# A hybrid decoder layer: first products on inputs that are not yet normed, and a readout placed later

## The reference, cut to what matters

```python
h = rmsnorm(x, g_pre_mix)                 # x * rsqrt(mean(x*x) + eps) * g
proj = einsum('btd,de->bte', h, w_in) + b_in
u_a, u_g, q, k, v, o, ig, fg, gate_conv, gate_m = split_in(proj)
u = u_a * sigmoid(u_g)                    # GLU, feeds a depthwise convolution of width 31
...
# per head (4): chunkwise mLSTM memory C (512 x 256), normaliser n, running max m,
# driven by the gate rows ig and log_sigmoid(fg)
hm = hm * rsqrt(mean(hm*hm) + eps) * g_mh * sigmoid(o)
mix = sigmoid(gate_conv) * y_conv + sigmoid(gate_m) * y_m
x = x + rmsnorm(mix @ w_o, g_post_mix)
ff = square(relu(rmsnorm(x, g_pre_ff) @ w_ff1 + b_ff1)) @ w_ff2 + b_ff2
x = x + rmsnorm(ff, g_post_ff)
```

## Time and profile before

| | us |
|---|---|
| median of 3 runs | 1249.0 (1248.9 to 1249.25) |
| profiled execution, its own time | 1248.76 |
| its span, first to last instruction | 1247.3 |
| TensorE busy in it | 1234.6 |
| VectorE, ScalarE busy | 717.3, 498.6 |
| first product matmul begins | 15.88 |
| last GLU chunk ends | 120.2 |

### The profile page before, as it was taken

The page is one execution under the profiler, slowest core; times in us unless marked ns, Lnnn a source line. Parts: engine busy times, 40 slices in busy tenths (PEclk is TensorE's granted clock), DMA queues, the critical chain, the costliest instruction groups (busy, mean ns, idle before and its releaser), DMA issues.

```text
span 1247.3 us, 23524 instructions
## 1 busy us (share of the span) xinstructions
PE 1234.6 (99%) x9043; PEld 1159.9 (93%) x9043; DVE 717.3 (58%) x1032; ACT 498.6 (40%) x764; POOL 62.5 (5%) x128
## 2 busy tenths in 40 slices
PE   8999999999999999999999999999999999999998
PEld 7999978888797888879999999999999999999998
DVE  6342678887877888788455443338453122443334
ACT  5332443453354335335543222247554223444221
POOL 4011001101100110110000000000000000000000
PEclk9999999999999999999999999999999999999999
DMA  6235316514450651442323222331323222223222
GB/s 207 79 119 180 105 34 237 202 44 163 172 181 34 235 196 50 154 177 77 99 85 102 85 84 84 145 105 43 112 91 101 85 84 85 84 85 101 85 67 72
DMA packets 40357, 141.23 MB, mean 113 GB/s; under 512 B 4804, under 2 KB 7236, under 8 KB 40184
## 3 DMA queue, kind: packets, MB, share of 16 engines
q1 hardware_dynamic: 28888, 99.37, 23.6%
q0 software_dynamic: 11424, 41.23, 9.4%
HBM read 118.31 MB, written 22.26 MB: 113 GB/s over the span
## 4 chain that ended last, share of the span: by engine, by line
PE 95%; DVE 1%; DMA 1%; ACT 1%; issue 0%; DVEq 0%; SPq 0%; POOL 0%; POOLq 0%; ACTq 0%
PE product L1542 88%; PE side L1542 7%; DMA out_c_s<-crg 1%; DMA x<-in_xT 1%; DVE crg L1253 0%; DVE accp L1133 0%; ACT sqh L755 0%; PE side L1700 0%; DMA crg<-in_c_in 0%; DVE hm L1277 0%; DVE sqacc L1282 0%; SPq L389 0%; ACT whi L559 0%; PE product L1690 0%; DVEq L1133 0%
## 5 line engine op out<-in xcount | busy, mean ns | idle before, releaser
L970 DVE TENSOR_TENSOR wlo<-wraw,whi 128x1024 fp32r<-128x1024 f32 x176 | 215.2, 1224 | 222.9 <-ACT whi L559 218.9
L1542 PE MATMUL product<-ahi,whi 128*128 128x256 f32 x1520 | 320.4, 290 | 4.1 <-DVE alo L995 3.9
L1542 PE MATMUL product<-ahi,wlo 128*128 128x256 f32 x1520 | 317.2, 288 | 0.0
L1542 PE MATMUL product<-alo,whi 128*128 128x256 f32 x1520 | 314.9, 287 | 0.0
L559 ACT ACTIVATE whi<-wraw 128x1024 fp32r<-128x1024 f32 x176 | 184.4, 1052 | 254.8 <-PE product L1542 183.9
L1542 PEld LDWEIGHTS product<-ahi,whi 128*128 128x128 f32 x1520 | 244.7, 188 | 11.8 <-issue 6.2
L1542 PEld LDWEIGHTS product<-alo,whi 128*128 128x128 f32 x1520 | 245.3, 188 | 0.0
L1542 PEld LDWEIGHTS product<-ahi,wlo 128*128 128x128 f32 x1520 | 243.9, 188 | 0.0
L1133 DVE SCALAR_TENSOR_TENSOR accp<-u,wdw,accp 128x512 f32<-128x512 f32 x240 | 163.4, 745 | 0.3
L1542 PE MATMUL product<-hidhi,whi 128*128 128x288 f32 (+1 forms) x512 | 111.2, 289 | 0.0
L1542 PE MATMUL product<-hidlo,whi 128*128 128x288 f32 (+1 forms) x512 | 110.8, 288 | 0.0
(11 more groups left out here) (297 smaller groups left out, 1599.8 us busy)
## 6 DMA issues: line engine op xcount, KB each, us to landing
wraw<-in_wstream SPq DMA_DIRECT2D x176, 512.0 KB, 3.4
crg<-in_c_in POOLq DMA_DIRECT2D x32, 512.0 KB, 6.6
out_c_s<-crg POOLq DMA_DIRECT2D x32, 512.0 KB, 2.9
hb<-head_rows POOLq DMA_DIRECT2D x4, 580.0 KB, 5.3
x<-in_xT SPq DMA_DIRECT2D x4, 544.0 KB, 5.1
sgm<-in_xT SPq DMA_DIRECT2D x1, 2176.0 KB, 8.3
out_c_p<-cst POOLq DMA_DIRECT2D x4, 512.0 KB, 8.2
out_yT<-y SPq DMA_DIRECT2D x4, 288.0 KB, 2.2
```

The source lines that it names most:

```text
L970: V.tensor_tensor(wlo[:, k % RING, :, :], wraw[:, k % 2, :, :], whi[:, k % RING, :, :].bitcast(f32), ALU.subtract).then_inc(lo_done, 1)
L1542: return pe.matmul(out, lhsT, rhs, start=start, stop=stop, skip_group_check=check)
```

## The change

- **Start.** New operands `ghi` and `glo` are the two parts of x * g, without the root. ScalarE makes `ghi` with `g_pre_mix` as its scale, VectorE `glo` in one instruction. They feed chunks 0 to 7 and the gate rows. The first weight chunk and `col` are loaded ahead of x, the second weight chunk after half of it.
- **Order on TensorE.** Twenty warm-up matmuls; then chunks 0 and 1 in turns of four, two and two tiles; chunk 2 goes into `side` and has the column sums of the squares behind its third tile. All squares are made by ScalarE and added by VectorE.
- **Eviction.** For chunks 0 to 7 VectorE multiplies the product by `rst` out of PSUM (`gate_scaled`, `up_scaled`), ScalarE takes the sigmoid from SBUF (`gated`), VectorE makes the GLU product from SBUF (`up_gated`). The gate rows are multiplied by `rst` in `gate_logits`.
- **Meanwhile** the normed operands `ahi` and `alo` are made in between; TensorE waits for all of them ahead of chunk 8. A sigmoid is taken once right behind the root for its table.
- **POOL** waits for chunk 7's end ahead of the first load of head rows, bias and states, since `ghi` and `glo` lie in that memory.
- **Heads.** `weighted(0)` runs ahead of `readout(1)`, with its square ahead of the chain of L736 and `update(4)` behind its sum; `pv0` and `cu4` swap places in `USES`, hence slots.

The diff, cut to its core (allocation, semaphore names and the removed helpers `operands`, `two_products` and `sum_of_squares` left out):

```diff
 
 USES = ["q0", "q1", "k0", "k1", "v0", "kts", "v1", "v2", "v3", "v4",
         "o0", "cu0", "cu1", "o1", "cu2", "cu3", "o2", "o3",
-        "cu4", "pv0", "cu5", "pv1", "cu6", "pv2", "cu7", "pv3"]
+        "pv0", "cu4", "cu5", "pv1", "cu6", "pv2", "cu7", "pv3"]
 USES_HEAD = len(USES) // 2
 
 BY_CHUNK = {"q0": 0, "q1": 1, "k0": 2, "k1": 3, "v4": 7, "o0": 8, "o1": 9, "o2": 10, "o3": 11}
@@ -206,6 +206,8 @@
         wkp = at("wkp", [P, ST], f32)
...
@@ -385,11 +389,16 @@
         @block.sync
         def _(sp):
             stream = wstream.rearrange("(n s) p k m -> n s p k m", s=2)
+
+            def first_chunk(s):
+                sp.dma_start(wraw[:, s, :, :], wstream[s, :, :, :]).then_inc(raw_in[s], 16)
+
+            first_chunk(0)
+            sp.dma_start(col[:, :], cols).then_inc(col_in, 16)
             for q in range(KT // 2):
                 sp.dma_start(x0[:, 2 * q:2 * q + 2, :], xT[:, 2 * q:2 * q + 2, :]).then_inc(x_in[q], 16)
-            sp.dma_start(col[:, :], cols).then_inc(col_in, 16)
-            for s in range(2):
-                sp.dma_start(wraw[:, s, :, :], wstream[s, :, :, :]).then_inc(raw_in[s], 16)
+                if q == 1:
+                    first_chunk(1)
...
-            pool.wait_ge(raw_in[1], 16)
+            pool.wait_ge(x_in[KT // 2 - 1], 16)
...
+            pool.wait_ge(chunk_done, KT)
             rows_load(0)
             bias_load(0)
             for n in range(C_RING):
...
             act.preload_act_table_set("natural_log_exp_and_others")
+            hi(0, 4, 0)
+            act.wait_ge(col_in, 16)
             for q in range(KT // 2):
                 act.wait_ge(x_in[q], 16)
-                act.activation(fr[:, q:q + 1, :], tile(x0, 2 * q), ACT.Square).then_inc(sq_ready, 2)
-            hi(0, 4, 0)
+                for j in (2 * q, 2 * q + 1):
+                    act.activation(tile(ghi, j), tile(x0, j), ACT.Copy, scale=c("g_pre_mix", j)).then_inc(ghi_ready, 1)
+                if q == 1:
+                    hi(0, 4, 1)
+            hi(0, 4, 2)
+            for j in range(KT):
+                squares(j, tile(x0, j), j % 4, 4)
+            hi(0, 4, 3)
             act.wait_ge(pool_step, 15)
-            root(1, sq_added, KT, table=False)
-            hi(0, 4, 1)
-            for j in range(KT):
-                if j == 4:
-                    hi(0, 4, 2)
-                operand(j, j, ahi)
+            root(1, x_stat, 1, table=False)
+            act.activation(warm[:, :], eps[:, :], ACT.Sigmoid).then_inc(table_in, 1)
+
+            def gated(j):
+
+                act.wait_ge(drained[0], j + 1)
+                if j > 0:
+                    act.wait_ge(u_full, j)
+                act.activation(sg[:, :], fr[:, 0, :], ACT.Sigmoid, bias=c("b_ug", j)).then_inc(sig_done, 1)
+
+            gated(0)
+            hi(0, 4, 4)
             act.wait_ge(gate_in, 48)
             act.activation(wghi[:, :, :], wg[:, :, :], ACT.Copy).then_inc(gw_hi, 1)
-
+            operand(0, 0, ahi)
+            operand(1, 1, ahi)
+            hi(0, 4, 5)
+            gated(1)
+            operand(2, 2, ahi)
+            operand(3, 3, ahi)
+            hi(0, 4, 6)
+            for j in range(4, KT):
+                operand(j, j, ahi)
...
-            glu(0)
-            glu(1, {0: (gate_exp, gate_log)})
+            for k in range(4):
+                hi(1, 4, k + 3)
+                if k % 2 == 0:
+                    gated(2 + k // 2)
+                if k == 0:
+                    gate_exp()
+                    gate_log()
+            act.wait_ge(u_full, 4)
             glu(2, {1: (gate_weights,), 3: (sample_operands,)})
             glu(3)
...
@@ -730,6 +771,19 @@
                         act.activation(npn[:, bass.ds(h, 1), :], side[:, 2:3, P:P + QT], ACT.Copy).then_inc(np_used, 1)
 
                 act.preload_act_table_set("natural_log_exp_and_others")
+
+                def weighted_square(k):
+                    s = use(f"pv{k}")
+                    if k >= 2:
+                        act.wait_ge(hsum_ready, VT * h + (k - 1))
+                    act.activation(sqh[:, k % 2, :], psum[s][:, 0, :], ACT.Square).then_inc(hsq_ready, 1)
...
+                weighted_square(0)
                 act.wait_ge(snum_ready, h + 1)
                 act.wait_ge(srec_ready, h + 1)
                 apart(act)
...
                 act.activation(hs[:, :], hs[:, :], ACT.Copy, scale=sst[:, 4:5]).then_inc(hs_norm, 1)
-
...
-                for k in range(VT):
-                    s = use(f"pv{k}")
-                    if k >= 2:
-                        act.wait_ge(hsum_ready, VT * h + (k - 1))
-                    act.activation(sqh[:, k % 2, :], psum[s][:, 0, :], ACT.Square).then_inc(hsq_ready, 1)
-                    if k == 1:
-                        state_out(0)
+                weighted_square(1)
+                state_out(0)
+                weighted_square(2)
+                weighted_square(3)
                 state_out(1)
...
+            def operand_scaled(j):
+
+                if j >= 2:
+                    dve.wait_ge(opnd_lo, j - 1)
+                V.scalar_tensor_tensor(fr[:, 2 + j % 2:3 + j % 2, :], tile(x0, j), c("g_pre_mix", j), rst3, ALU.mult,
+                                       ALU.mult).then_inc(tile_ready, 1)
+
+            def operand_pair(j):
+
+                if j + 1 < KT:
+                    operand_scaled(j + 1)
+                dve.wait_ge(opnd_hi, j + 1)
+                V.tensor_tensor(tile(alo, j), fr[:, 2 + j % 2:3 + j % 2, :], tile(ahi, j).bitcast(f32),
+                                ALU.subtract).then_inc(opnd_lo, 1)
+
+            def gained_lo(j):
+
+                dve.wait_ge(ghi_ready, j + 1)
+                V.scalar_tensor_tensor(tile(glo, j), tile(x0, j), c("g_pre_mix", j), tile(ghi, j).bitcast(f32), ALU.mult,
+                                       ALU.subtract).then_inc(glo_ready, 1)
+
             lo(0, 4, 0)
             dve.wait_ge(col_in, 16)
+            for j in range(KT):
+                gained_lo(j)
+                if j == 3:
+                    lo(0, 4, 1)
+            lo(0, 4, 2)
+            dve.wait_ge(sq_ready, 2)
+            V.tensor_tensor(sqs[:, :], fr[:, 0, :], fr[:, 1, :], ALU.add).then_inc(sq_added, 2)
+            for j in range(2, KT):
+                add_square(j, j % 4)
+            lo(0, 4, 3)
             dve.wait_ge(root_ready, 1)
-            operands(0, x0, "g_pre_mix", ahi, alo, {0: lambda: lo(0, 4, 1), 3: lambda: lo(0, 4, 2)})
+
+            def gate_scaled(j, src):
+
+                dve.wait_ge(chunk_done, 2 * j + 1)
+                if j > 0:
+                    dve.wait_ge(sig_done, j)
+                V.tensor_tensor(fr[:, 0:1, :], src, rst3, ALU.mult).then_inc(drained[0], 1)
+
+            def up_scaled(j):
+
+                dve.wait_ge(chunk_done, 2 * j + 2)
+                if j > 0:
+                    dve.wait_ge(u_full, j)
+                V.tensor_tensor(fr[:, 1:2, :], slot(1), rst3, ALU.mult).then_inc(drained[1], 1)
+
+            def up_gated(j):
+
+                dve.wait_ge(drained[1], j + 1)
+                dve.wait_ge(sig_done, j + 1)
+                V.scalar_tensor_tensor(u[:, j, HIST:HIST + SEQ], fr[:, 1, 0:SEQ], c("b_ua", j), sg[:, 0:SEQ], ALU.add,
+                                       ALU.mult).then_inc(u_done, 1)
+                new = u[:, j, HIST + SEQ:].rearrange("p (b r) -> p b r", r=SROW)[:, :, HIST:SROW]
+                V.scalar_tensor_tensor(new, fr[:, 1, SEQ:TT].rearrange("p (b t) -> p b t", t=DEC_T), c("b_ua", j),
+                                       sg[:, SEQ:TT].rearrange("p (b t) -> p b t", t=DEC_T), ALU.add, ALU.mult).then_inc(u_full, 1)
+
+            gate_scaled(0, slot(0))
+            up_scaled(0)
+            operand_scaled(0)
+            operand_scaled(1)
+            up_gated(0)
+            lo(0, 4, 4)
             dve.wait_ge(gw_hi, 1)
             V.tensor_tensor(wglo[:, :, :], wg[:, :, :], wghi[:, :, :].bitcast(f32), ALU.subtract).then_inc(gw_lo, 1)
+            dve.wait_ge(opnd_hi, 1)
+            V.tensor_tensor(tile(alo, 0), fr[:, 2:3, :], tile(ahi, 0).bitcast(f32), ALU.subtract).then_inc(opnd_lo, 1)
+            operand_pair(1)
+            gate_scaled(1, spare())
+            lo(0, 4, 5)
+            operand_pair(2)
+            operand_pair(3)
+            up_scaled(1)
+            up_gated(1)
+            lo(0, 4, 6)
+            for j in range(4, KT):
+                operand_pair(j)
 
...
-                n = mark(V.tensor_scalar(row["fg"][:, :], across(side[32:36, 0:2, :]), bg[32:36, :], None, ALU.add))
+                n = mark(V.tensor_tensor(sqs[0:36, :], across(side[0:36, 0:2, :]), rst[0:36, :], ALU.mult))
+                dve.wait_ge(dve_step, n)
+                n = mark(V.tensor_scalar(row["fg"][:, :], sqs[32:36, :], bg[32:36, :], None, ALU.add))
                 dve.wait_ge(dve_step, n)
                 V.scalar_tensor_tensor(row["ex"][:, :], row["fg"][:, :], -1.0, row["fg"][:, :], ALU.mult, ALU.min).then_inc(fx_ready, 1)
```

(77 more changed lines are left out.)

58 lines of the change are left out of this document (15 added, 43 removed).

## The result

The changed kernel takes 1252.18 us in the median of 7 runs (1250.33 to 1253.84) where the kernel before, run beside it, takes 1248.88 us: a ratio of 1.0027, 95% interval 1.0017 to 1.0037. The prediction was 1241.2 us and faster; the result is 3.3 us slower, 11.0 us away from the forecast. The profiled execution took 1251.81 us with a span of 1250.3.

What follows compares the result with a forecast made beforehand. The prediction took TensorE, busy 99% of the span, as the bound. Start 9.0 gained, chunk 7's wait 3.3 lost, heads 2.1 gained make 7.8 us off 1249.0: 1241.2 us, range 1237.7 to 1244.3.

Steps and rivals of the forecast that it cites:

- What else is moved costs nothing: From the start to the head: POOL's moved loads of `hist`, rows and states delay nothing, 0 us.
- The start: Before the gated unit's chunk 4: first product at 8.3 us instead of 15.88, no half clock, chunk 4 9.0 us ahead.
- The wait at chunk 7: Near 57 us TensorE waits on a VectorE row product behind ScalarE's gate-row stretch: 3.3 us lost, 2.3 to 4.3.
- The prediction's sum for VectorE's queue: From the root at 25.3 us, VectorE's work up to chunk 4's row product takes 25.2 us, ending near 50.3.
- the Trainium skill's price with a drain: At chunk 7: a drain with each of ScalarE's two table switches adds 2.8 us, making the wait 6.0; not adopted.
- The rival of the falling clock: TensorE's clock falls to half in the new 3.3 us gap, 1.7 us more lost: 1242.9 us; chance 0.26.
- The heads: In the four heads, reordering removes the state load wait, `hm` waits and some `crg` waiting: 2.1 us gained, 1.2 to 3.2.

Runs made afterwards that it cites:

- experiment 5: The changed kernel with 92 idle VectorE instructions (waits on a semaphore raised long ago) ahead of the head loop: 1243.32 us, ratio 0.9954.
- Experiment 3: The kernel before with 27 idle VectorE instructions ahead of the head loop and no other difference: 1257.78 us, ratio 1.0068.
- experiment 2: The changed kernel with the edits of the head loop taken back, so the new start alone: 1252.50 us, ratio 1.0036.
- experiment 6: The changed kernel, chunk 8's weights rounded before the gate rows' exponential and logarithm, VectorE's gate steps behind its row products, no padding: 1251.44 us, ratio 1.0021.
- experiment 7: The changed kernel with both the new order of experiment 6 and the 92 idle instructions of experiment 5: 1239.30 us, ratio 0.9919.
- experiment 1: The kernel before with the edits of the head loop alone, nothing changed ahead of the loop: 1246.76 us, ratio 0.9978.
- experiment 8: The kernel before with 7 idle VectorE instructions ahead of the head loop, a single run: 1263.43 us.
- experiment 10: The kernel before with 20 idle VectorE instructions ahead of the head loop, a single run: 1259.08 us.
- experiment 11: The kernel before with 50 idle VectorE instructions inside the head loop and none ahead of it: 1258.96 us, ratio 1.0076.
- experiment 9: The kernel before with 13 idle VectorE instructions ahead of the head loop, a single run: 1261.82 us.

## Why the prediction was wrong

**The step that failed** is the one between the parts: from the start to the head "What else is moved costs nothing", and the three heads after the first priced by TensorE's and VectorE's waits alone. The change adds 27 instructions to VectorE ahead of a loop whose body, as far as these runs show, just fits what VectorE holds of its instructions, and the prediction put nothing for them. The runs put its price at 8.9 us (experiment 5 against the changed kernel), by distances 2.5, 2.7 and 3.9 us at the three passages (111.56 − 109.05, 111.57 − 108.92, 112.79 − 108.94). The last holds a fall of the clock as well (the windows at 464, 465 and 466 us have 0.54, 0.50 and 0.50), which is 1.7 us of these 9.0; the stands themselves are some 7.3. The term was not mis-sized, it was missing, and neither a rival nor the range held it. Experiment 3 has it on the kernel before, with nothing else changed.

**The start, right in its order, about a microsecond late.** The first product came at 9.29 us, not 8.3: x landed 1.0 us later than reckoned (7.41, the end of the chain's 5.44 us, against 6.4); why is not shown, but the reckoning had no term for `col` ahead of it. The twenty warm-ups ran to 8.6. Chunk 2 began at 21.59 (20.4), the column sums at 23.86 with no wait, the row product at 26.47 right behind the root (25.3), and chunk 4 at 40.54 (39.3), 7.6 us ahead of the kernel before, whose timeline has it at 48.17, where 9.0 were forecast. The clock was 1.00 through this stretch, so the 3.4 us at half clock of the earlier trace rows did go.

**The wait at chunk 7, right in its mechanism and place.** TensorE waits on the row product of L1074 until 60.85. VectorE's and ScalarE's rows are those of the working: `whi` at 55.22 behind the logarithm, `wlo` at 56.20 (57.1 reckoned as its end, measured 57.4), the decay, the row product at 59.98 (59.8). The wait was 2.0 instead of 3.3, since TensorE itself came 1.6 us later (58.8 for 57.2) and VectorE's row only 0.35 (60.85 for 60.5). That is why the start's missing 1.4 us cost almost nothing in the end: VectorE's chain set the time at which chunk 7 began. (The prediction's sum for VectorE's queue, 25.3 + 25.2, is 50.5 and not 50.3, which changes nothing.) By the Trainium skill's price with a drain ("ScalarE: Activation LUTs", What ACT_TABLE_LOAD costs) the wait would have been longer. The trace has two table loads of 1.28 us and two passes of 0.66 from 51.30 to 55.22, 3.88 of 3.92 us, so no drain of 1.38 us stands between them.

**The rival of the falling clock came true** (its chance was put at 0.26). After the stop the half-microsecond windows of the changed kernel (stretch, busy times, then granted clock) read:

```profile
61.00:61.50 0.50, 0.50 (x4) 0.50 (x5) 0.50 (x2) 0.00 (x0) 0.00 (x0) 0.80 0.00 0
61.50:62.00 0.50, 0.50 (x4) 0.50 (x4) 0.50 (x2) 0.26 (x1) 0.28 (x1) 0.50 0.00 0
...
64.00:64.50 0.50, 0.50 (x5) 0.50 (x4) 0.50 (x1) 0.00 (x0) 0.00 (x0) 0.50 0.49 139
64.50:65.00 0.50, 0.50 (x5) 0.50 (x5) 0.47 (x3) 0.00 (x0) 0.00 (x0) 0.79 0.94 377
```

0.80, six at 0.50, 0.79: 3.4 us at 1.2 GHz and 1.7 us lost, the same as in the earlier trace rows, behind 2.0 us of waiting instead of 3.9. But it is not certain: the profiled runs of experiments 2 and 5 waited 2.0 and 2.1 us at the same place and kept 1.00. A stop and its fall together cost 3.6 us in the profiled runs of the changed kernel and experiment 6 (225.02 − 221.44), and 4.0 in the medians of experiments 5 and 7.

**The heads, right**: 2.1 us forecast, 2.7 measured (experiment 1, interval 1.6 to 3.9). The waits for `hm` and the load went, the four for `crg` stayed at 0.3.

**The rest of the sum.** Chunk 4 7.6 ahead, 2.0 for the wait, 1.7 for the clock leaves 3.9 up to the heads (the stretch that begins at 60.85 ends at 116.56, 3.6 us ahead of the end of the one in the earlier trace rows, 120.17); head 0 ends 4.2 ahead. Without the missing term and with the rival's fall the prediction's own account gives 1242.9. Experiment 5 measured 1243.3 in the median, and its profiled execution, which has no fall, 1242.45 where the sum without a fall says 1241.2. So the other steps held to 1 or 2 us each. The start's missing 1.4 us came back as 1.3 us less of waiting, and the heads gave 0.6 more; against that, between 1 and 2 us stay unexplained, 0.7 of them behind the last head (690.1 us in the profiled run of experiment 5 for 689.4). That the total comes as near as this is in part luck. The step that was left out, the fetch, cost more than the 7.8 us that all the others together were to win.

## What to carry to other kernels

Before adding or removing instructions ahead of a long hardware loop, count the instructions of its body and of what stands ahead on each engine, and look at the instruction queue's packets in the profile: packets during a loop's later turns, with a stand of that engine marked "issue" at each turn, mean that the loop is fetched anew. Idle instructions ahead of the loop (92 here), in time in which the engine waits anyhow, can move it back to where it fits; in another kernel that computes the same thing as few as 7 cost 1.1% (a single run), and 27 cost 0.7%. And when a change gains time ahead of such a loop, compare the distance from turn to turn, not only the total: it showed here at once that the gain was real and the loss was somewhere else.

A stop of TensorE can be worth more than its length. In the profiled executions, 6 of the 22 stops of 2.0 to 2.5 us had a fall of the clock within 2 us of their end, 1.7 us lost each, and equal kernels scattered by 3.5 us (the changed kernel) to 8.5 (experiment 6). With the last such stop removed it was 1 us.

## What the runs showed of the hardware

- VectorE's instructions come in packets of 8192 bytes. A loop body of 342 instructions was not fetched again in its later turns when it began 103 instructions into the built program, with five packets in each turn at 110, 116, 123, 130 and 258, and again with none at 222. Four blocks of 128 with one of them fetched ahead is the simplest account that fits all of these and the body of 392; how many are held was not measured by itself, and the program's start has a part that the built program doesn't show, which the account leaves free.
- The price of such a turn is a stand of 4.1 to 5.0 us of VectorE at the jump, 2.1 to 3.0 us of TensorE's waiting, and, apart from the clock, 7 to 9 us of the kernel's time for three jumps.
- The granted clock fell to half behind stops of TensorE, in some executions and not in others. By the length of the stop, in the profiled executions, a fall came during it or within 2 us of its end: 6 of 22 of 2.0 to 2.5 us, 6 of 9 of 2.5 to 3.0, 7 of 7 of 3.9 (at the start of the old order). It stayed down for 3.4 us or 6.8 us: behind the 3.9 us at the start it was 3.4 in the kernel before and experiments 8, 10 and 11, and 6.8 in experiments 1, 3 and 9.
